# Gate rows of a conditioned decoder layer: one 256-column product a token, ScalarE and VectorE share the copy

## The reference

```python
def peer(h, w_q_peer, sub_keys1, sub_keys2, u_emb, v_emb):
    ...
        qh = (xc @ w_q_peer).astype(F32).reshape(PEER_CHUNK, PEER_HEADS, 2, PEER_HALF)
        s1 = jnp.einsum('chd,kd->chk', qh[:, :, 0], sub_keys1.astype(F32))
        s2 = jnp.einsum('chd,kd->chk', qh[:, :, 1], sub_keys2.astype(F32))
        v1, i1 = lax.top_k(s1, PEER_TOPK)
        v2, i2 = lax.top_k(s2, PEER_TOPK)
        ...
        eid = jnp.take_along_axis(cand_id, top_j, axis=-1)
        gate = jax.nn.softmax(top_s, axis=-1)
        act = jax.nn.gelu(jnp.einsum('chkd,cd->chk', u_emb[eid], xc).astype(F32))
        return jnp.einsum('chk,chkd->cd', (gate * act).astype(v_emb.dtype), v_emb[eid])
```

## Time and profile before

| | us |
|---|---|
| median of 3 runs | 1407.49 (1406.44 to 1407.97) |
| profiled execution, its own time | 1407.39 |
| its span in the trace | 1405.6 |
| outside the span | 1.8 |

### The profile page before, as it was taken

One profiled execution on the slowest core, in us unless ns is written; L12 is line 12 of the kernel. 1 busy time (PEld: TensorE's weight loads), 2 busy tenths in 40 slices (PEclk: granted clock), 3 DMA queues, 4 the chain that ended last, 5 costly groups with the idle time before them and its releaser, 6 DMA issues.

```text
span 1405.6 us, 30010 instructions
## 1 busy us (share of the span) xinstructions
PE 1337.5 (95%) x9976; PEld 1253.2 (89%) x9976; DVE 976.6 (69%) x2130; ACT 592.3 (42%) x932; POOL 767.8 (55%) x335
## 2 busy tenths in 40 slices
PE   5999999889989999799999999999999999999996
PEld 3777677767879999789999999999999999999996
DVE  2499923965435999992666565650788888888886
ACT  1200234355434444554444444444444444444442
POOL 0200023520655477786655556557777777777774
PEclk8999999889998999999999999999999999999998
DMA  8776454234443456455545545456666666666663
GB/s 315 275 244 204 146 201 160 89 126 139 147 158 106 136 180 207 145 176 192 168 159 166 168 162 168 159 166 223 220 211 210 210 210 211 212 211 212 215 211 134
DMA packets 103750, 258.37 MB, mean 184 GB/s; under 512 B 12496, under 2 KB 52144, under 8 KB 103312
## 3 DMA queue, kind: packets, MB, share of 16 engines
q1 hardware_dynamic: 94144, 245.81, 52.0%
q10 hardware_dynamic: 8752, 8.93, 1.9%
q0 software_dynamic: 800, 2.91, 0.6%
HBM read 234.60 MB, written 23.00 MB: 183 GB/s over the span
## 4 chain that ended last, share of the span: by engine, by line
PE 87%; DVE 4%; issue 3%; POOL 2%; DMA 2%; ACT 1%; ACTq 0%; SPq 0%; POOLq 0%; DVEq 0%
PE ps L1868 28%; PE ps L1821 9%; PE ps L1476 9%; PE ps L1814 9%; PE ps L1815 8%; PE ps L1849 5%; PE ps L1513 4%; PE ps L1519 4%; PE ps L1525 3%; POOL split L596 2%; DMA ring<-in_stream 2%; PE ps L1536 1%; PE ps L1457 1%; PE ps L1799 1%; PE ps L1596 1%
## 5 line engine op out<-in xcount | busy, mean ns | idle before, releaser
L596 POOL TENSOR_TENSOR split<-ring,split 128x1024 fp32r<-128x1024 f32 x256 | 629.5, 2461 | 274.2 <-ACT split L869 274.0
L1868 PE MATMUL ps<-h2r,split 128*128 128x288 f32 x3072 | 406.4, 294 | 0.9 <-ACT h2r L931 0.9
L1868 PEld LDWEIGHTS ps<-h2r,split 128*128 128x128 f32 x3072 | 406.2, 188 | 1.1 <-ACT x L898 1.1
L869 ACT ACTIVATE split<-ring 128x1024 fp32r<-128x1024 f32 x256 | 270.4, 1057 | 205.7 <-PE ps L1868 204.1
L1436 DVE TENSOR_TENSOR h2r<-x,h2r 128x288 fp32r<-128x288 f32 x128 | 298.8, 2335 | 76.5 <-ACT h2r L931 76.5
L1814 PE MATMUL ps<-h2r,split 128*128 128x288 f32 x1024 | 284.9, 305 | 5.2 <-ACT split L869 5.2
L1815 PE MATMUL ps<-h2r,split 128*128 128x288 f32 x1024 | 278.8, 296 | 0.0
L561 POOL TENSOR_TENSOR split<-ring,split 128x1024 fp32r<-128x1024 f32 x48 | 118.7, 2475 | 179.1 <-ACT split L667 179.0
L1814 PEld LDWEIGHTS ps<-h2r,split 128*128 128x128 f32 x1024 | 193.9, 189 | 5.8 <-ACT split L869 3.8
L1815 PEld LDWEIGHTS ps<-h2r,split 128*128 128x128 f32 x1024 | 193.5, 189 | 0.0
L1821 PE MATMUL ps<-h2r,split 128*128 128x288 f32 x1024 | 165.3, 304 | 6.7 <-POOL split L596 6.4
(11 more groups left out here) (240 smaller groups left out, 1349.1 us busy)
## 6 DMA issues: line engine op xcount, KB each, us to landing
ring<-in_stream SPq DMA_DIRECT2D x391, 512.0 KB, 3.3
act_dram<-x SPq DMA_DIRECT2D x128, 144.0 KB, 1.8
x<-act_dram SPq DMA_DIRECT2D x128, 144.0 KB, 3.0
big<-in_cache_k ACTq DMA_DIRECT2D x16, 128.0 KB, 3.3
big<-in_cache_v ACTq DMA_DIRECT2D x16, 128.0 KB, 3.2
x<-in_xT ACTq DMA_DIRECT2D x1, 1152.0 KB, 7.9
x_dram<-x ACTq DMA_DIRECT2D x1, 1152.0 KB, 5.2
big<-x_dram SPq DMA_DIRECT2D x1, 1152.0 KB, 5.0
```

The lines of the kernel that those rows point to most:

```text
L596: nc.gpsimd.tensor_tensor(split[:, n % 2, 1], ring[:, slot_of(n), :], split[:, n % 2, 0].bitcast(f32), ALU.subtract).then_inc(lo_ready, 1)
L869: nc.scalar.activation(split[:, n % 2, 0], ring[:, slot_of(n), :], ACT.Copy).then_inc(hi_ready, 1)
L1868: ins = MM(ps[k][:, 0:T], v[v_part][:, k], wr[:, n % 2, w_part], start=start, stop=stop)
```

## The change

Each gate is cut into a high part, rounded to f32r by ScalarE as it copies the picks (line 917, third row), and a low part, one VectorE subtraction into a fourth row of `parts`. `hot1` becomes two matrices side by side, [128, 2, 128], high and low, written in f32r by one scalar_tensor_tensor over 256 elements in place of a tensor_scalar over 128. `hot2` keeps its instruction and is written as f32r. TensorE does one f32r product of 256 columns a token in place of a float32 product of 128 columns. A bank now holds two tokens, so that banks 2 to 5 are used, two a block. ScalarE copies the high halves of each pair (256 elements, twice a block), and VectorE adds the low halves from PSUM to what ScalarE wrote in `gate_mat` (`gate_sum`, 256 elements, twice a block, for the block before). `gate_copied` is now counted a pair and comes from VectorE; a new semaphore `gate_high` goes from ScalarE to VectorE. The buffers move: `x`, `mod` and others are freed ahead of the gates and the memory is given to `parts`, `act`, `gate2`, `hot1` and `hot2`; `gate2` is a copy of the part of `mod` that is still needed at the end.

```diff
-        late_x = x[:, :, :].rearrange("p k t -> p (k t)")
-        parts = late_x[:, 0:3 * T].rearrange("p (a t) -> p a t", t=T)
...
+        parts = sb("parts", 4, T)
+        act = sb("act", 2, T)
+        gate2 = sb("gate2", KC, NG)
+        hot1 = sb("hot1", NHOT, 2, P, dt=f32r)
+        hot2 = sb("hot2", NHOT, P, dt=f32r)
+        act_bs = [parts[:, n] for n in range(R)]
...
-            sp.wait_ge(gate_copied, MIXED)
+            sp.wait_ge(gate_copied, 2 * MIXED)
...
                     if tokens4:
-                        eng.wait_ge(hot_used, g * (2 * R) + 2 * (n + 1 - BEFORE))
-                        nc.scalar.activation(gate_mat[:, :, bass.ds(g * (4 * R) + 4 * (n - BEFORE), 4)],
-                                             ps[2 + n % 2][:, :].rearrange("p (t i) -> p i t", t=4), ACT.Copy)\
-                            .then_inc(gate_copied, 1)
+                        for pair in range(2):
+                            eng.wait_ge(hot_used, g * (2 * R) + (2 * (n - BEFORE) + pair + 1))
+                            both = ps[2 + 2 * (n % 2) + pair][:, :].rearrange("p (t a i) -> p a i t", t=2, a=2)
+                            nc.scalar.activation(gate_mat[:, :, bass.ds(g * (4 * R) + (4 * (n - BEFORE) + 2 * pair), 2)],
+                                                 both[:, 0], ACT.Copy).then_inc(gate_high, 1)
...
-                nc.scalar.activation(parts[:, n], pa[n][:, 0:T], ACT.Copy).then_inc(picks_copied, 1)
+                nc.scalar.activation(parts[:, n].bitcast(f32r) if n == 2 else parts[:, n], pa[n][:, 0:T], ACT.Copy)\
+                    .then_inc(picks_copied, 1)
...
+            step(V.tensor_copy(gate2[:, :, :], mod[:, 5]))
+            V.tensor_tensor(parts[:, 3], pa[2][:, 0:T], parts[:, 2], ALU.subtract).then_inc(gate_cut, 1)
+            dve.wait_ge(gate_cut, 1)
+            settle()
+
             def one_hot(token, slot):
                 col = bass.ds(token, 1)
-                V.tensor_scalar(hot2[slot], iota_ps, parts[:, 1, col], None, ALU.is_equal)
-                return V.tensor_scalar(hot1[slot], iota_ps, parts[:, 0, col], parts[:, 2, col],
-                                       ALU.is_equal, ALU.mult)
-
-            def token_pairs(g, first=False):
+                V.tensor_scalar(hot2[:, slot], iota_ps, parts[:, 1, col], None, ALU.is_equal)
+                return V.scalar_tensor_tensor(hot1[:, slot], iota_ps.unsqueeze(1).to_broadcast([P, 2, P]),
+                                              parts[:, 0, col], parts[:, 2:4, col].to_broadcast([P, 2, P]),
+                                              ALU.is_equal, ALU.mult)
+
+            def gate_sum(g, pair, odd):
+
+                both = ps[2 + 2 * odd + pair][:, :].rearrange("p (t a i) -> p a i t", t=2, a=2)
+                gates = gate_mat[:, :, bass.ds(g * 4 + 2 * pair, 2)]
+                dve.wait_ge(gate_high, g * 2 + (pair + 1))
+                V.tensor_tensor(gates, both[:, 1], gates, ALU.add).then_inc(gate_copied, 1)
+
+            def token_pairs(g, odd, first=False):
                 for pair in range(2):
                     if not first:
 
                         dve.wait_ge(hot_used, g * 2 + (pair - 1))
                     for j in range(2):
                         last = one_hot(g * 4 + (2 * pair + j), 2 * pair + j)
                     last.then_inc(hot_ready, 1)
...
+                    if not first:
+                        gate_sum(g - 1, pair, 1 - odd)
...
             def gate_tokens(q, n, pair, first=False):
 
-                if pair == 0 and not first:
-
-                    pe.wait_ge(gate_copied, q - 1)
+                if not first:
+
+                    pe.wait_ge(gate_copied, q * 2 + (pair - 3))
                 pe.wait_ge(hot_ready, q * 2 + (pair + 1))
-                for s in (2 * pair, 2 * pair + 1):
-                    last = MM(ps[2 + n % 2][:, s * P:(s + 1) * P], hot2[s], hot1[s], start=True, stop=True)
+                for j in range(2):
+                    s = 2 * pair + j
+                    last = MM(ps[2 + 2 * (n % 2) + pair][:, j * 2 * P:(j + 1) * 2 * P], hot2[:, s],
+                              hot1[:, s].rearrange("p a i -> p (a i)"), start=True, stop=True)
                 last.then_inc(hot_used, 1)
```

More of the change, by code:

```diff
@@ L172, in sem @@
             return ctx.enter_context(nc.semaphore(name))
[L175 to L181, removed]
         ring = sb("ring", R, D)
@@ L188, in build, with sb_early @@
         big = sb("big", NBIG)
+        with ExitStack() as before_gates:
+            def sb_early(name, *shape, dt=f32):
+                return before_gates.enter_context(nc.sbuf_tensor(name, [P] + list(shape), dt))
+            x = sb_early("x", KC, T)
+            mod = sb_early("mod", 6, KC, NG)
+            scl = sb_early("scl", 2, KC, NG)
+            ident = sb_early("ident", P)
+            ones = sb_early("ones", P)
+            iota = sb_early("iota", P, dt=bf16)
+            gnorm = sb_early("gnorm", 2, KC)
+            m_row2 = sb_early("m_row2", 2, P)
         gate_mat = big[:, :].rearrange("p (i t) -> p i t", t=T)
@@ L447, in build @@
         gate_copied = sem("gate_copied")
+        gate_cut = sem("gate_cut")
+        gate_high = sem("gate_high")
         gelued = sem("gelued")
@@ L504, in _ @@
             for n in range(R):
-                sp.dma_start(act_b[:, n], act_dram[n]).then_inc(act_loaded[n], 16)
+                sp.dma_start(act_bs[n], act_dram[n]).then_inc(act_loaded[n], 16)
             with sp.Fori(NSUB // R - 2, NSUB // R) as g:
@@ L515, in _ @@
                     sp.wait_ge(w_lo, g * R + (n + 1))
-                    sp.dma_start(act_b[:, n], act_dram[bass.ds(g * R + (n + R), 1)].rearrange("o p t -> (o p) t"))\
+                    sp.dma_start(act_bs[n], act_dram[bass.ds(g * R + (n + R), 1)].rearrange("o p t -> (o p) t"))\
                         .then_inc(act_loaded[n], 16)
@@ L930, in v_turn @@
                         eng.wait_ge(o_done, g * R + (n - 1))
-                    nc.scalar.activation(wr[:, n % 2, 0], act_b[:, n], ACT.Copy).then_inc(w_hi, 1)
+                    nc.scalar.activation(wr[:, n % 2, 0], act_bs[n], ACT.Copy).then_inc(w_hi, 1)
                     m = (n + 1) % R
@@ L1259, in _, with residual @@
             settle()
-            def residual(k, src, which, xin, dst, tmp, done):
-                V.scalar_tensor_tensor(dst[:, k, 0:TP], src[0], mod[:, which, k, 0:1], xin[:, k, 0:TP],
+            def residual(k, src, gain, xin, dst, tmp, done):
+                V.scalar_tensor_tensor(dst[:, k, 0:TP], src[0], gain[:, k, 0:1], xin[:, k, 0:TP],
                                        ALU.mult, ALU.add).then_inc(done, 1)
-                V.tensor_tensor(seq(tmp), seq(src[1]), mod[:, which, k, 1:NG].unsqueeze(2).to_broadcast([P, NSEQ, TD]),
+                V.tensor_tensor(seq(tmp), seq(src[1]), gain[:, k, 1:NG].unsqueeze(2).to_broadcast([P, NSEQ, TD]),
                                 ALU.mult).then_inc(done, 1)
@@ L1274, in _ @@
                 bank = lin[BANK[key]]
-                residual(n, (bank[:, 0:TP], bank[:, TP:T]), 2, x, x, bank[:, TP:T], x1_ready)
+                residual(n, (bank[:, 0:TP], bank[:, TP:T]), mod[:, 2], x, x, bank[:, TP:T], x1_ready)
             hs = h2[:, :, TP:T].rearrange("p k (b t) -> p k b t", t=TD)
@@ L1415, in token_pairs @@
                     last.then_inc(hot_ready, 1)
[L1417 to L1422, removed]
+                    if not first:
+                        gate_sum(g - 1, pair, 1 - odd)
+            token_pairs(0, 0, True)
+            token_pairs(1, 1)
+            with dve.Fori(1, MIXED // 2) as g:
+                for odd in range(2):
+                    token_pairs(g * 2 + odd, odd)
+            for pair in range(2):
+                dve.wait_ge(hot_used, 2 * (MIXED - 1) + pair + 1)
+                gate_sum(MIXED - 1, pair, 1)
+            dve.wait_ge(gate_copied, 2 * MIXED)
             def weights(g, behind):
@@ L1426, in weights @@
                     dve.wait_ge(act_loaded[n], g * 16 + 16)
-                    V.tensor_tensor(act_b[:, n], act_b[:, n],
+                    V.tensor_tensor(act_bs[n], act_bs[n],
                                     gate_mat[:, bass.ds(g * R + n, 1)].rearrange("p o t -> p (o t)"), ALU.mult)\
@@ L1435, in low @@
                 dve.wait_ge(w_hi, c + 1)
-                V.tensor_tensor(wr[:, n % 2, 1], act_b[:, n], wr[:, n % 2, 0].bitcast(f32), ALU.subtract)\
+                V.tensor_tensor(wr[:, n % 2, 1], act_bs[n], wr[:, n % 2, 0].bitcast(f32), ALU.subtract)\
                     .then_inc(w_lo, 1)
@@ L1446, in _ @@
                 dve.wait_ge(bank_done, k + 1)
-                residual(k, (ps[k][:, 0:TP], ps[k][:, TP:T]), 5, xe, ye, dtmp, y_out)
+                residual(k, (ps[k][:, 0:TP], ps[k][:, TP:T]), gate2, xe, ye, dtmp, y_out)
         @block.tensor
@@ L1885, in _ @@
             pe.wait_ge(gelued, NSUB)
-            pe.wait_ge(gate_copied, MIXED)
+            pe.wait_ge(gate_copied, 2 * MIXED)
             for n in range(R):
```

## The result

The changed kernel takes 1377.4 us (median of 4 runs, 1376.5 to 1377.8) against 1407.57 (1406.44 to 1407.97): a ratio of 0.9788, 95% interval 0.9775 to 0.980. The forecast was 1377.7. The profiled execution took 1376.5, its span is 1374.7.

What follows compares the result with a forecast made beforehand. TensorE was taken to pace the mixed stage; 0.41 us less a block, 72 times, is 29.7 us, so 1407.4 - 29.7 = 1377.7 us, other parts hidden. Range 1373 to 1393, the forecast's own 1374 to 1382.

Steps and rivals of the forecast that it cites:

- What bounds the stage: Mixed stage: TensorE paces it, busy for all of its 293 us; the gates cost 0.89 us a block.
- TensorE's part: Gate products: four f32r of 0.120 us replace eight records of 0.11; block 3.68 us, not 4.09; 29.7 us less.
- VectorE's part: Mixed block: one-hots 2.64 us plus sums 0.70 make 3.34 against 3.68, so VectorE stays under TensorE, 0.34 to spare.
- rival 1: Mixed stage: VectorE paces it, block up to 3.88 us, gain only 15 us, time 1392; chance 0.12.
- The new wait: VectorE's gate_sum between the one-hots of pairs 0 and 1 waits for ScalarE's high copy; 0.9 us to spare.
- The edges: Stage start: under 0.8 us more on VectorE, hidden by 14 us; end: last sums about 2 us later, 38 us cover.
- Rival 2: Mixed stage: GpSimd's subtraction holds VectorE's gate_sum or new hot1; VectorE's block 4.75 us, time 1455; chance 0.06.
- Rival 3: Gate product: f32r at 256 columns no cheaper than float32, 0.44 us a token, time 1471; chance 0.04.
- Rival 4: Behind the stage: the gain is given back because something there follows another clock; about 1407; chance 0.03.

Runs made afterwards that it cites:

- the runs with 64, 128 and 192 columns: Changed kernel with an extra f32r product a token of 64 columns (1410.19 us) or 192 (1409.21 us), or its 256-column product split into two of 128 (1408.88 us).
- the high part alone: Changed kernel with one f32r product of 128 columns a token, high part of the gates only, no sums on VectorE: 1377.01 us.
- the run without idle time: Changed kernel with two more one-hot instructions of 128 elements a mixed block on VectorE, one in each pair: 1384.96 us.

## Why the prediction was right

**What bounds the stage** held. Doubling TensorE's products lengthens the block by 0.43 us, taking VectorE's sums away changes nothing, one more VectorE instruction changes nothing, and the changed kernel's trace has no wait of TensorE ahead of a gate product.

**TensorE's part, 0.120 us a product and 3.68 us a block,** measured 0.12 and 3.69. The number was right, and its reasoning was not the whole of it. I scaled the price by columns. That holds at 256 columns and fails below: the runs with 64, 128 and 192 columns show a least time of 0.11 us for a product with its own weight load of 128 columns. By columns, two products of 128 would have given 1381, and 1409 was measured. That 256 columns lie just over this least time, where the price by columns still holds, I did not know.

The format has its share too, and the kernel before shows how much. An earlier stage has plain float32 products of 288 and 264 columns, at a granted clock of 1.00:

```profile
129.62 2.10 PE L1476 MATMUL ps<-big,ring 128*128 128x288 f32 x8
131.56 3.72 PE L1596 MATMUL ps<-big 128*128 128x264 f32 x16
```

Eight float32 records of 288 columns take 1.94 us, 0.24 each, where an f32r record takes 0.13. Records of 256 columns (line 1680) start 0.22 us apart, of 128 columns 0.11. A float32 product is two records, so my estimate for one of 256 columns is 0.44 us, where f32r took 0.12. The gain is then made of two steps. In f32r a product of 128 columns is one record of 0.11 in place of two, as the high part alone shows. The low part's 128 columns ride beside it for about 0.01. One record a token less is 288 x 0.11 = 31.7 us; less that 0.01 a token, 29 us, against 29.4 measured.

The Trainium skill, TensorE: Matmul & The Clock Gate, section LDWEIGHTS (loading the stationary operand), gives a weight load as the columns of the stationary operand divided by 1.2 GHz, from which I estimate 0.107 us for 128. The distance of the loads above, 0.11 to 0.12, and the measured least time of 0.11 agree with it, while the record of a load lasts 0.19. That it is the load itself, and not something else that comes once with each load, is not shown: no run had a gate product with fewer stationary columns.

**VectorE's part, 3.34 us a block:** 3.26, as the run without idle time shows. hot1 0.39 (forecast 0.40), sum 0.33 (0.35). The slack from start to start was 0.43 us, not 0.34, and the kernel is by 0.09 us further from rival 1. The strided pattern of the sum costs nothing that can be seen: busy 0.427 us at the median, where line 1248's contiguous 288 elements took 0.46 and 256 would be 0.41 to 0.43 by my estimate. I took two rules of the Trainium skill (Advanced Engine Details and Errata, sections SBUF Cachelines and PSUM Cachelines) as a warning for this pattern, the first one wrongly. It asks for at least two accesses to a line, and the sum's pairs of neighbouring elements in `gate_mat` give it those. The second one does describe the sum's reading of PSUM with a step of 256, though it speaks of matmuls first; no slowdown of VectorE shows in the 0.427 us, and the measurement decides.

**The new wait** is there and is where I put it: ScalarE's copy ends VectorE's idle time in 72 blocks, 24.7 us in all, 0.34 a block (counted from an instruction's end, so it is less than the slack from start to start). It costs the time next to nothing: the kernel with the high part alone has neither the wait nor the sums, and its block is 0.01 us shorter.

**The edges:** the first one-hot ran at 639.96, the first gate product at 653.8, 14 us of cover as forecast. The two VectorE instructions ahead of it took 0.6 us.

**Where luck helped.** The forecast met the time to 0.3 us, which is finer than the method. The stage gave 29.4 us; the medians differ by 30.2, and the rest is spread ahead of the stage. On another chip the same two kernels differed by 29.8 at times 2 us higher.

**The rivals.** Rival 1 didn't decide, and begins where it was said to, a little later. Rival 2 doesn't arise with one input in PSUM; with both of hot1's in SBUF it costs 1493.6 - 1377.4 = 116 us, more than the 78 that the forecast's average gave, since in every block one hot1 is held to the end of the subtraction. The Trainium skill's rule (SBUF — State Buffer, section Who interferes with whom) is borne out by this pair of runs. Rival 3 was far off: 0.12 us for the f32r product against the 0.44 of its price. What is true in it is only that a record of 128 columns costs 0.11 in either format. Rival 4 didn't come: blocks behind the stage last 3.20 us as before.

## What to carry to other kernels

Count products with their own weight load of 128 columns before columns: up to 256 columns of f32r a product cost 0.11 to 0.12 us here, so a correction term set beside the main term in one product is nearly free, and as a product of its own costs as much as the main one. When work moves to an engine with slack, sum its instructions from start to start against the pacing engine's block; here 0.43 us of slack took one instruction of 0.26 and not two. Keep one tensor input of VectorE in PSUM while GpSimd works on SBUF: 0.47 us here, against up to 2.62 with both in SBUF.

## What the runs showed of the hardware that I had not expected

An extra f32r product of 64 columns lengthens the block by as much as one of 192, 0.11 us, although the next product starts 0.03 us behind it. The products of 288 columns in the changed kernel don't keep one distance: one line's eight took 1.05 to 1.07 us from start to the next line's start, and sixteen high products 2.16 us in one block of the changed kernel (802.75 to 804.91) and 2.11 in one with doubled gate products (801.83 to 803.94), both at a granted clock of 1.00. What sets this is open; no run was made for it.
